# Both feed-forward layers of a two-layer encoder as seven block products, in one stage each

## The reference

```
h = rmsnorm(x, g2)
f = (silu(h @ w_gate) * (h @ w_up)) @ w_down
x = x + rmsnorm(f, g3)
```

## Time and profile before

| | us |
|---|---|
| median of 3 runs | 3339.05 (3337.58 to 3340.87) |
| the profiled execution, its span | 3339.0 |
| PE busy | 3030.5 (91%) |
| DVE busy | 1309.2 (39%) |
| ACT busy | 922.7 (28%) |
| POOL busy | 688.4 (21%) |

### The profile page before, as it was taken

One profiled execution on the slowest core, in us unless ns is written; L12 is line 12 of the kernel. 1 busy time (PEld: TensorE's weight loads), 2 busy tenths in 40 slices (PEclk: granted clock), 3 DMA queues, 4 the chain that ended last, 5 costly groups with the idle time before them and its releaser, 6 DMA issues. The chain is left out here.

```text
span 3339.0 us, 46381 instructions
## 1 busy us (share of the span) xinstructions
PE 3030.5 (91%) x17722; PEld 1804.8 (54%) x17722; DVE 1309.2 (39%) x2062; ACT 922.7 (28%) x1744; POOL 688.4 (21%) x681
## 2 busy tenths in 40 slices
PE   6899888999999997788988888988868999999997
PEld 3565554666665665445545454555444666665664
DVE  4354344111111113677557556566565111111113
ACT  4233233222221112334225214323333222221111
POOL 3001023111110003344125215314413111010002
PEclk9999998999999999889989999999978999999998
DMA  3100232111111113110220110111131111111113
GB/s 115 48 23 23 33 101 82 44 44 44 44 44 50 43 50 122 45 54 7 70 67 1 64 51 29 51 38 54 42 110 62 44 44 44 44 46 47 45 53 111
DMA packets 78969, 178.30 MB, mean 53 GB/s; under 512 B 15217, under 2 KB 43505, under 8 KB 78705
## 3 DMA queue, kind: packets, MB, share of 16 engines
q1 hardware_dynamic: 78832, 176.50, 16.5%
HBM read 147.53 MB, written 28.94 MB: 53 GB/s over the span
## 5 line engine op out<-in xcount | busy, mean ns | idle before, releaser
L149 PE MATMUL f_gu<-x_hi,w_hi 128*128 128x384 f16 x2112 | 692.6, 328 | 10.0 <-POOL x_lo L510 9.4
L150 PE MATMUL f_gu<-x_lo,w_hi 128*128 128x384 f16 x2112 | 692.7, 328 | 0.0
L151 PE MATMUL f_gu<-x_hi,w_lo 128*128 128x384 f16 x2112 | 692.5, 328 | 0.0
L133 DVE SCALAR_TENSOR_TENSOR w_lo<-w_raw,w_hi 128x1024 f16<-128x1024 f32 (+1 forms) x151 | 199.4, 1320 | 744.6 <-ACT w_hi L122 744.6
L149 PE MATMUL f_dn<-f_mid_hi,w_hi 128*128 128x384 f16 x1056 | 346.0, 328 | 11.5 <-PEq L93 11.5
L150 PE MATMUL f_dn<-f_mid_lo,w_hi 128*128 128x384 f16 x1056 | 346.0, 328 | 0.0
L151 PE MATMUL f_dn<-f_mid_hi,w_lo 128*128 128x384 f16 x1056 | 345.8, 327 | 0.0
L1356 POOL TENSOR_TENSOR f_mid_lo<-f_gu_mid,f_mid_hi 128x384 f32 x132 | 120.5, 914 | 879.4 <-ACT f_mid_hi L1328 879.4
L149 PEld LDWEIGHTS f_gu<-x_hi,w_hi 128*128 128x128 f16 x2112 | 208.0, 98 | 156.0 <-POOL x_lo L510 11.6
L151 PEld LDWEIGHTS f_gu<-x_hi,w_lo 128*128 128x128 f16 x2112 | 207.7, 98 | 138.8 <-issue 3.6
L150 PEld LDWEIGHTS f_gu<-x_lo,w_hi 128*128 128x128 f16 x2112 | 207.5, 98 | 135.5 <-issue 2.0
(11 more groups left out here) (360 smaller groups left out, 5369.3 us busy)
## 6 DMA issues: line engine op xcount, KB each, us to landing
w_raw<-in_gate_up SPq DMA_DIRECT2D x88, 512.0 KB, 3.5
w_raw<-in_ssm_w SPq DMA_DIRECT2D x56, 512.0 KB, 3.6
w_raw<-in_down SPq DMA_DIRECT2D x32, 704.0 KB, 4.0
mid_x<-y SPq DMA_DIRECT2D x18, 768.0 KB, 4.3
w_raw<-in_ab_w_in SPq DMA_DIRECT2D x18, 512.0 KB, 3.5
ss_state<-in_state SPq DMA_DIRECT2D x32, 256.0 KB, 3.7
out_new_state<-ss_state SPq DMA_DIRECT2D x32, 256.0 KB, 2.3
f_dn_tail_xr<-mid_x SPq DMA_DIRECT2D x8, 768.0 KB, 5.4
```

What stands on the lines that cost most here:

```text
L133: self.nc.vector.scalar_tensor_tensor(self.w_lo[:, u % 2, 0:cols], self.w_raw[:, u % 2, 0:cols], WSCALE, self.w_hi[:, u % 2, 0:cols], ALU. ...
L149: self.nc.tensor.matmul(out, wh, xh, start=(first and k == 0), stop=False)
L150: self.nc.tensor.matmul(out, wh, xl, start=False, stop=False)
L151: mm = self.nc.tensor.matmul(out, wl, xh, start=False, stop=(last and k == k_tiles - 1))
```

## The change

Both stages of a feed-forward become one, `feed_forward`, with an order of work written out by `Plan`. Operands are cut in two by two blocks: tokens into two groups g of 576 with two halves of 288 each, the inner dimension into two halves, the outputs into two (gate and up for the first layer, two output tiles for the second). Seven block products of sums of blocks replace eight (the list PRODUCTS: weights A11, A12, A22, S1 to S4 with activations B11, B21, B22, T1 to T4).

- A "gu" set is one of 22 steps for one group: 7 products x 4 k-tiles x 3 matmuls of 288 columns. A "d" set is one of 20 tasks (5 chunks of 512 middle rows x 4 pairs of output tiles) for one group: 7 x 2 x 3 matmuls of 288. The last two middle tiles are a "plain" task, 24 x 2 x 3 matmuls of 384 columns.
- Order: four gu steps (both groups each), then the d sets of that chunk (pair 0 and 1 of group 0, then of group 1, then pair 2 and 3, both groups each), five times; then gu steps 20 and 21, then the plain task. Down's sums accumulate in y over chunks.
- Within a set VectorE, ScalarE and GpSimd form the sums U between products from PSUM: products 3, 4, 5, 6 start when p1 (ScalarE), q (VectorE), p5 (ScalarE), u (VectorE) are there, since they go into banks that these free.
- Weight blocks come as one load of 2 MB (gu) or 1 MB (d); GpSimd forms S1 to S4 (`weight_sums`), ScalarE the high parts in two instructions (3 and 4 blocks), VectorE the low parts in two (`weights_lo`); this happens in the sets of the task before.
- After each odd gu step of a group, T1 to T4 of the middle values are formed, then their high parts (`mid_hi`, 2,016 columns, ScalarE) and low parts (`mid_lo`, 1,152 on VectorE and 864 on GpSimd), in the program of the next set.
- The input is staged in eight parts e (pair of k-tiles and group): `x_stage`, `x_sums`, `x_hi`, `x_lo`. Parts 0 to 3 stand ahead of set 0, 4 and 5 in set 0, 6 and 7 in set 1. All three blocks' residuals and norms stand ahead of part 0.
- The previous stages no longer load and split the first units (`load_ring` ends at end - 4); SP loads the first two tasks ahead of the x loads. Squares of the output are taken at the plain task for all 24 tiles; GpSimd adds those of blocks 0 and 1.
- The loops are unrolled. Weights are laid out in memory by task.

```diff
         def _(sp):
-            load_ring(c, sp, s, end - 2)
+            load_ring(c, sp, s, end - 4)
...
-            c.load_weights(sp, end + 2)
-            c.load_weights(sp, end + 3)
...
-                    if b == BLOCKS - 1:
-                        c.split_hi(act, end, 0, acc_ready, 6 * i + 5)
...
+CHUNKS = 5
+GU_COLS = KD // 2 * P
+D_COLS = 2 * P
+A11, A12, A22, S1, S2, S3, S4 = range(FORMS)
+B11, B21, B22, T1, T2, T3, T4, B12 = range(FORMS + 1)
+PRODUCTS = ((A11, B11, 0), (S2, T2, 1), (S1, T1, 2), (A12, B21, 0), (S3, T3, 1), (S4, B22, 2), (A22, T4, 1))
...
+            load(0)
+            load(1)
             lead.sync(sp)
-            load_ring(c, sp, s, s + 2 * FT)
...
+                else:
+                    parts = lambda k, lo, f: mf[:, k, g, lo, f, :]
+                    ready = plan.event_of(2 * ch + 1, g)
+                    pe.wait_ge(mhi_ready, ready)
+                    pe.wait_ge(mlo_pool, ready)
+                    pe.wait_ge(mlo_dve, ready)
+                for k, (f, form, which) in enumerate(PRODUCTS):
+                    if k == 0:
+                        pe.wait_ge(hi_done, 2 * w + 1)
+                        pe.wait_ge(lo_done, 2 * w + 1)
+                    elif k == 1:
+                        pe.wait_ge(hi_done, 2 * w + 2)
+                        pe.wait_ge(lo_done, 2 * w + 2)
+                    if k < 3:
+                        banks_free(n, k)
+                    else:
+                        pe.wait_ge((p1_ready, q_ready, p5_ready, u_ready)[k - 3], n + 1)
+                    one(bank[3 * plan.banks(n) + which][:, 0:HALF], w, f, parts, plan.cols(w) // P, form, k < 3)
+
+            if early:
...
+                    act.wait_ge(products, plan.all_of(used))
+                act.wait_ge(m3_ready, e + 1)
+                act.wait_ge(m4_ready, e + 1)
+                nc.scalar.copy(parted(pair, g, 0), mid[:, g, 0:FORMS]).then_inc(mhi_ready, 1)
+
+            def product_set(n):
+                kind, w, g, _, ch = sets[n]
+                s, p = plan.banks(n), n % 2
+                x, z = bank[3 * s][:, 0:HALF], bank[3 * s + 2][:, 0:HALF]
+                scale = 1.0 if kind == "gu" else 1 / WSCALE
+                act.wait_ge(products, plan.product(n, 0))
+                if n >= 2:
+                    act.wait_ge(set_done, n - 1)
+                nc.scalar.activation(p1[:, p], x, AF.Copy, scale=scale).then_inc(p1_ready, 1)
+                if n and set_event(n - 1) is not None:
+                    mid_hi(set_event(n - 1))
+                for v in range(1, len(tasks)):
+                    if plan.at[v] == n:
+                        weights_hi(v, 0)
+                act.wait_ge(products, plan.product(n, 2))
+                nc.scalar.activation(p5[:, p], z, AF.Copy, scale=scale).then_inc(p5_ready, 1)
...
+            def x_stage(e):
+                g, k = divmod(e, 4)
+                buf = staged[g][k % 2]
+                if e >= 2:
+                    same = e - 2 if e not in (4, 5) else 3
+                    dve.wait_ge(xhi_ready, same + 1)
+                    dve.wait_ge(xlo_pool, same + 1)
...
+                                                      lead.rms_x.banks[b][:, lo - b * BW:hi - b * BW], ALU.mult, ALU.mult)
+                ins.then_inc(xb_ready, 1)
...
+            def weights_late(n):
+                for w in range(1, len(tasks) - 1):
+                    if plan.s_after[w] == n and plan.at[w] == n:
+                        weights_lo(w, 1)
+
+            def gu_set(n):
+                _, w, g, st, _ = sets[n]
+                s, p = plan.banks(n), n % 2
+                y, z = bank[3 * s + 1][:, 0:HALF], bank[3 * s + 2][:, 0:HALF]
+                dve.wait_ge(products, plan.product(n, 1))
+                dve.wait_ge(p1_ready, n + 1)
...
+                if n and set_event(n - 1) is not None:
+                    mid_lo(set_event(n - 1))
+                weights_between(n)
+                dve.wait_ge(products, plan.product(n, 4))
+                v_.tensor_tensor(u[:, p], y, p1[:, p], ALU.add).then_inc(u_ready, 1)
+                weights_late(n)
+                if n < 2:
+                    x_lo(4 + 2 * n)
+                    x_sums(5 + 2 * n)
+                dve.wait_ge(products, plan.product(n, 5))
+                dve.wait_ge(q_ready, n + 1)
+                v_.tensor_tensor(q[:, p], z, q[:, p], ALU.add).then_inc(z_done, 1)
+                dve.wait_ge(products, plan.product(n, 6))
...
+                dve.wait_ge(products, plan.product(n, 1))
+                dve.wait_ge(p1_ready, n + 1)
+                v_.scalar_tensor_tensor(q[:, p], y, 1 / WSCALE, p1[:, p], ALU.mult, ALU.add).then_inc(q_ready, 1)
+                if set_event(n - 1) is not None:
+                    mid_lo(set_event(n - 1))
+                weights_between(n)
+                dve.wait_ge(products, plan.product(n, 3))
...
+                dve.wait_ge(products, plan.product(n, 4))
+                v_.scalar_tensor_tensor(u[:, p], y, 1 / WSCALE, p1[:, p], ALU.mult, ALU.add).then_inc(u_ready, 1)
+                weights_late(n)
+                dve.wait_ge(products, plan.product(n, 5))
...
+            weights_lo(0, 0)
+            x_stage(0)
+            x_stage(1)
+            x_sums(0)
+            lead.rms_x.inverses(dve, 2)
+            x_lo(0)
+            x_stage(2)
+            x_sums(1)
...
+            g_ = nc.gpsimd
+
+            def weight_sums(w):
+                a21, a11, a12, a22 = (raw(w, k) for k in range(4))
+                s1, s2, s3, s4 = (summed(w, k) for k in range(4))
+                pool.wait_ge(raw_loaded[w % 2], 16 * (w // 2 + 1))
+                if w:
+                    pool.wait_ge(hi_done, 2 * w)
+                    pool.wait_ge(lo_done, 2 * w)
+                g_.tensor_tensor(s1, a21, a22, ALU.add).then_inc(sum_step, 1)
+                g_.tensor_tensor(s3, a11, a21, ALU.subtract)
+                pool.wait_ge(sum_step, 2 * w + 1)
+                g_.tensor_tensor(s2, s1, a11, ALU.subtract).then_inc(sum_step, 1)
+                pool.wait_ge(sum_step, 2 * w + 2)
+                g_.tensor_tensor(s4, a12, s2, ALU.subtract).then_inc(sums_done, 1)
...
+            def product_set(n):
+                kind, w, g, k, ch = sets[n]
+                p = n % 2
+                if n and set_event(n - 1) is not None:
+                    mid_lo(set_event(n - 1))
+                if n < 2:
+                    x_sums(4 + 2 * n)
+                    x_sums(5 + 2 * n)
+                    x_lo(4 + 2 * n)
+                if kind == "d" and ch:
+                    pool.wait_ge(p1_ready, n + 1)
+                    g_.tensor_tensor(s0[:, p], p1[:, p], out_tile(k, 1, g, 0), ALU.add).then_inc(c21_ready, 1)
+                    pool.wait_ge(q_ready, n + 1)
+                    g_.tensor_tensor(q[:, p], q[:, p], out_tile(k, 0, g, 1), ALU.add).then_inc(c12_ready, 1)
+                pool.wait_ge(u_ready, n + 1)
+                pool.wait_ge(p5_ready, n + 1)
+                g_.tensor_tensor(u[:, p], u[:, p], p5[:, p], ALU.add).then_inc(c22_ready, 1)
+                if n < 2:
+                    x_lo(5 + 2 * n)
+                if kind == "gu" and k // 2 < 2 * CHUNKS:
+                    pool.wait_ge(set_done, n + 1)
+                    if k % 2:
+                        g_.tensor_tensor(mid[:, g, T3], mid[:, g, B22], mid[:, g, B12], ALU.subtract
+                                         ).then_inc(m3_ready, 1)
+                    else:
+                        g_.tensor_tensor(mid[:, g, T1], mid[:, g, B12], mid[:, g, B11], ALU.subtract
+                                         ).then_inc(m1_ready, 1)
```

More of the change, by code:

```diff
@@ L1350, in _ @@
+            add_square(dve, v_, 2, KD - 1)
+            tail.residual(dve, 1, range(KD))
         @block.gpsimd
         def _(pool):
[L1352 to L1357 removed]
```

639 lines of the change are left out of this document (532 added, 107 removed).

## The result

The changed kernel takes 3463.78 us (median of 4 runs, 3460.92 to 3465.22), the kernel before 3339.84 (4 runs, 3337.58 to 3340.87): 1.037 times as long, 95% interval 1.0354 to 1.0383. The profiled execution has a span of 3462.8 us, 123.8 more than before. The direction was forecast, the size was not: 3405, with a range up to 3455.

The account below looks back on a forecast made before the run. TensorE, busy throughout gate/up and down, was taken as the bound. Matmuls -180.4, seam -15.4, lead +96.8, tail +26.6 and stalls +140 gave +67.6 on 3339.0: 3406.6, stated as 3405 us, range 3285 to 3455.

Parts of the forecast that it names:

- the lead: Before each layer's first products: residuals, norms and four staged pairs delay TensorE, 48.4 us a layer, +96.8 for both.
- the stalls: Inside gate/up and down sets: products wait for sums and splits, 66 plus 4 for clock, 70 us a layer, +140.
- Matmuls: TensorE in gate/up and down: 122.5 ns at 288 columns, 90.2 us less a layer, -180.4 for both.
- rival D: Gate/up and down matmuls don't shrink with their columns, from 139 ns at 288 nothing is gained: 3587 us; chance 0.02.
- the other estimate: Matmul time by the Trainium skill's issue-gap rule: 102 ns at 288 columns, 114 at 384, giving 3627 us.
- The seam: Between gate/up and down: the 5.92 us gap and down's cold start both go, 15.4 us less for both layers.
- 8 us a pair: In the lead: staging, sums and low parts charged one after another, 7.6 us, 8 with hand-overs, per k-tile pair.
- Rival B: In the lead: staging overlaps other engines, 5 us a pair, sets 0 and 1 30 us: 3362 us; chance 0.15.
- the other 35 down sets lose 0.1: 3.5: Down sets other than each chunk's first: 0.1 us lost in each, 3.5 us a layer.
- the first gate/up set after down: Its weights are split within the last down sets, so it loses 2.5 us, five times a layer: 12.5.
- Rival C: VectorE and GpSimd are full in every down set, +30 us a layer: 3465 us; chance 0.13.
- The tail: After the last product: squares and residuals on GpSimd, TensorE goes on 23.3 us after its end, +26.6 for both layers.

Follow-up runs that it names:

- e7: Changed kernel with block 0's residual moved behind block 2's output tiles in VectorE's program in the plain task: 3458.96 us.
- e5: Changed kernel with ScalarE copying product 0 between PSUM banks, TensorE accumulating onto it, GpSimd's adds and some of VectorE's gone: 3469.40 us.
- e8: e6 with instructions reordered on ScalarE and VectorE, e7's residual move and one extra matmul ahead of each layer's first product: 3354.67 us.
- e10: e8 with further reordering of weight splits, copies and event sums, and some lead work moved from VectorE to GpSimd: 3358.94 us.
- e13: e11 with two edits undone: GpSimd shares the middle rows' low parts again, and its weight sums no longer wait for VectorE's: 3330.01 us.
- e1: Changed kernel with all low parts of x and the middle rows on VectorE, none on GpSimd: 3456.43 us.
- e2: Changed kernel with u ahead of low parts on VectorE and, in down sets, product 2's copy ahead of rounding on ScalarE: 3446.49 us.
- e11: e8 with more reordering, middle rows' low parts on VectorE alone, GpSimd's weight sums after odd steps waiting for VectorE's sums: 3305.24 us.
- e6: e5 with the lead's staging, sums and low parts on VectorE alone: 3429.03 us.

## Why the prediction was off

Of 56 us that the forecast lacks, three terms hold more than all: the plain task, put at nothing (23.7), the lead (21.4) and the stalls (19.4).

**Matmuls, right.** 122.5 ns at 288 columns and 162.5 at 384, so -180.4 as forecast; rival D is out. So is the other estimate: the Trainium skill, "TensorE: Matmul & The Clock Gate", section "Back-to-back issue gap", led to 102 ns at 288 columns, and the trace disagrees with 122.5. **The seam** is gone, and it was worth 20.9 us, not 15.4: before, down's stretches lasted 3.9 and 5.1 us longer than 1,584 matmuls need, since they held 24 matmuls more, the tail's norm; these now stand in the plain task.

**The lead, too small: +96.8 forecast, +118.2 measured.** Layer 0: VectorE's first low part of the weights, the low parts of the third pair on both engines and of the fourth on GpSimd, and TensorE's two waits:

```profile
522.50 1.76 DVE L1697 SCALAR_TENSOR_TENSOR f_wlo<-f_raw,f_whi 128x1536 f16<-128x1536 f32 x1 [1.96 <-ACT f_whi L1583]
...
552.61 1.36 DVE L1725 TENSOR_TENSOR f_xf<-f_mid,f_xf 128x1152 f16<-128x1152 f32 x1 [1.99 <-ACT f_xf L1589]
...
552.66 2.99 POOL L1917 TENSOR_TENSOR f_xf<-f_mid,f_xf 128x864 f16<-128x864 f32 x1 [1.39 <-ACT f_xf L1589]
560.70 2.99 POOL L1917 TENSOR_TENSOR f_xf<-f_mid,f_xf 128x864 f16<-128x864 f32 x1 [5.05 <-ACT f_xf L1589]
...
563.78 0.40 PE L1480 MATMUL f<-f_xf,f_whi 128*128 128x288 f16 x1 [28.35 <-POOL f_xf L1917]
...
606.93 0.40 PE L1480 MATMUL f<-f_xf,f_whi 128*128 128x288 f16 x1 [10.01 <-POOL f_xf L1917]
```

Set 3 starts at 619.28; less three sets of 10.3 that is an effective start of 588.4 against 530.0, 58.4 lost; in layer 1 at 2684.05, 2653.2, which is 122.2 behind 2531.0, of which 62.4 came with it from layer 0 (1386.20 against 1323.80): 59.8. The mechanism holds, and what failed are the sizes of its steps, 10 us a layer in all. Staging starts 2.4 us late, as VectorE first waits 1.96 for the weights' high part, which was not priced. The four pairs with the last low part take 39.5 us in place of 37: "8 us a pair" is 8.5 (8.0 the last), since staging waits for GpSimd's low part of the pair before the last, 2.99 us beside VectorE's 1.36, and GpSimd forms the first task's sums (5.05 us) ahead of the first pair's, which was not priced either. Sets 0 and 1 take 43.15 in place of 40, with 10.01 of idle time for GpSimd's last low part at their end, and set 2 loses 2.1 where nothing was charged. Rival B (5 us a pair, 30 for the two sets) is refuted by the same rows.

**The stalls, +140 forecast, 159.4 measured** (79.5 and 79.9 from set 3 on, by the starts of the matmuls): the chain is right where the prediction followed it, and the near sum is in part luck. In layer 0 the set after an odd step loses 1.96 (1.9), all gate/up sets behind odd steps 20.7 (24), the first down set 4.85 (5.2), 24.2 in all (26). The step that failed is "the other 35 down sets lose 0.1: 3.5": they lose 34.6 a layer, the last four of each chunk 26.0 and the second 8.6, most of that at half clock. Against this, "the first gate/up set after down", charged 12.5, loses nothing: the next task's weights are split within the last down sets, and it is those that wait. Steps at half clock (240 ns in place of 122.5, at a granted clock of 0.50) hold 10.3 of the 79.5, where 4 were charged on top. So 31 us a layer too little in one term stand against some 22 too much in others. Rival C's time, 3465, was hit within 1.3 us, but that is luck: its late down sets are there, yet the third and fourth down set of each chunk lose nothing, so that the two engines are not full in every down set, and the rest of the miss is the lead and the plain task.

**The plain task, put at nothing.** It lasts 13.6 and 10.1 us longer than its matmuls; I took 2.8 and put it into the sum nowhere. TensorE waits there for the tail's norm, whose matmuls stand among the plain ones in its program:

```profile
1339.84 0.83 PE L226 MATMUL f<-consts,acc 128*128 128x1 f32 x6 [1.46 <-POOL acc L1417]
...
1360.33 1.65 PE L243 MATMUL f<-consts,f_tail_post_inv 128*128 128x128 f32 x6 [5.99 <-DVE f_tail_post_inv L238]
...
1360.11 0.17 DVE L238 RECIPROCAL f_tail_post_inv<-f_tail_post_root 128x3 f32<-128x3 f32 x1
```

VectorE's inverse for that norm (L238) stands behind the output sums, the squares' sums and the residuals of the last block. The two waits, 3.4 us of the 24 norm matmuls themselves and 2.4 at half clock are 13.2 of the 13.6 in layer 0; in layer 1 the wait for the inverse is 3.42. In e7, which moves the residual, it is 0.34 in layer 0 and none in layer 1.

**The tail, right:** TensorE goes on 22.7 and 22.5 us after the plain task (23.3), +10.9 and +14.2, 25.1 in place of 26.6. The weight loads are half of what is said above, 1,024 KB for a gate/up task and 512 for a down task in the profile; nothing was charged for them, and no group of products waits for one.

The terms measured are -180.4 - 20.9 + 118.2 + 159.4 + 23.7 + 25.1 = +125.1 against 123.8 in the spans; 1.3 us of this reckoning are not placed.

Order and sharing act together. Less work for the two engines, without the later orders (e5), gives nothing; the later orders, without keeping the engines apart, give only part (e8, e10, e13). How much of the changed kernel's own stalls the order or the turns alone could remove, without ScalarE's copy into PSUM, was not tried beyond e1 and e2, and e13's two edits were not undone one by one.

## What to carry to other kernels

Fewer matmuls are paid for in short instructions on other engines, and these must come within the time of a product. List for each product what releases it, and see what stands before that on its engine: no bulk work (splits of weights, low parts) belongs between. Then see which bulk work of VectorE and GpSimd runs at the same time: work for which nothing waits can still make the short instructions of a chain three times as long (0.46 and 1.41 us here), and a wait that keeps it back may gain time.

## What the runs showed of the hardware

The slowing is uneven, and a short instruction that meets a long one pays most. VectorE's sum of 288 columns goes from 0.46 us to 1.41 beside GpSimd, GpSimd's of 512 from 1.28 only to 1.49 there; but beside VectorE's low part of 2.69 us in e11 GpSimd's sum takes 3.29. VectorE's weights' low part of 2,048 columns goes from 2.28 to 3.91 beside one GpSimd instruction of 3.00. VectorE's u, which reads PSUM, kept its time through all of this in the changed kernel (L1767 and L1818, 453 and 449 ns in the mean, none above 460). A copy by ScalarE from PSUM to PSUM takes 0.38 us for 288 columns, and TensorE goes on accumulating onto what it wrote: e8 and e10 to e13 form their sums so. In e5 and e6 part of the second layer's result is lost; e8 adds, beside its orders, one matmul of 288 columns that begins the bank ahead of each layer's first product, and the result is whole. That it was product 0 of the second layer's first set that was lost fits this, but no run shows it by itself.
